# The attention steps of a two-layer hybrid block start inside its projection, with transposed probability tiles and row-group scores

## The reference

```python
h = rmsnorm(x, norm_mix[l]); proj = h @ w_in[l]                 # 15 chunks of 128 columns in the kernel
ua, cq, ckv, kr, qc, kc, vc, ud = split(proj)
ya = conformer_conv(ua, ...)     # gate, 31-tap causal depthwise conv, layernorm, silu, matmul
yb = mla(cq, ckv, kr, ...)       # 4 heads: q (96 wide) from cq, k and v from ckv, causal softmax
yc = diff_attention(qc, kc, vc, ...)  # 4 heads, each two maps of 32 columns:
#   sc = q.k * scale + bias(head, distance); a = softmax(sc); p = a[map 0] - lam * a[map 1]; p @ v; rmsnorm
yd = multiscale_pool(ud, ...)    # windows of 2, 4, 8, 16
x = x + concat(ya, yb, yc, yd) @ w_out[l]
x = x + memory_cross_attention(rmsnorm(x), mem, ...)   # k = m @ wk and v = m @ wv need mem alone
x = x + conv_glu_ffn(rmsnorm(x), ...)
```

## Time and profile before

| what | us |
|---|---|
| median of 3 runs | 1741.35 (1737.64 to 1742.45) |
| the profiled execution's own time | 1740.95 |
| its span, first to last instruction | 1739.2 |
| mean granted TensorE clock | 0.977 |
| PE busy | 1626.3 (94%) |
| DVE busy | 1104.0 (63%) |
| ACT busy | 706.7 (41%) |
| POOL busy | 235.1 (14%) |

### The profile page before, as it was taken

The page is one execution under the profiler, slowest core; times in us unless marked ns, Lnnn a source line. Parts: engine busy times, 40 slices in busy tenths (PEclk is TensorE's granted clock), DMA queues, the critical chain, the costliest instruction groups (busy, mean ns, idle before and its releaser), DMA issues. The chain is left out here.

```text
span 1739.2 us, 22473 instructions
## 1 busy us (share of the span) xinstructions
PE 1626.3 (94%) x7664; PEld 1279.8 (74%) x7664; DVE 1104.0 (63%) x1604; ACT 706.7 (41%) x1082; POOL 235.1 (14%) x212
## 2 busy tenths in 40 slices
PE   6889989889999999999998999988999999999996
PEld 3567687668767888888876768657867788888874
DVE  8967974775445764764764886485444674575575
ACT  3232345763334432432442335674243442342343
POOL 5510511112012000000020150112102000000002
PEclk9889999999999999999998999999999999999998
DMA  3143133322212233323224224241211333332323
GB/s 135 47 155 97 61 121 98 103 67 89 81 36 86 97 95 93 96 94 95 94 86 134 83 73 132 78 129 52 94 49 63 95 97 96 97 96 90 99 80 109
DMA packets 50048, 159.69 MB, mean 92 GB/s; under 512 B 6576, under 2 KB 6832, under 8 KB 49072
## 3 DMA queue, kind: packets, MB, share of 16 engines
q1 hardware_dynamic: 49968, 158.63, 29.4%
HBM read 144.97 MB, written 7.34 MB: 88 GB/s over the span
## 5 line engine op out<-in xcount | busy, mean ns | idle before, releaser
L675 ACT ACTIVATE wh<-raw 128x1024 fp32r<-128x1024 f32 x246 | 260.9, 1061 | 657.5 <-PE psum L1235 646.3
L1233 PE MATMUL psum<-a_hi,wh 128*128 128x512 f32 x1072 | 423.1, 395 | 7.8 <-DVE wl L927 7.2
L927 DVE TENSOR_TENSOR wl<-raw,wh 128x1024 fp32r<-128x1024 f32 x246 | 302.7, 1231 | 189.6 <-ACT wh L675 189.4
L1234 PE MATMUL psum<-a_lo,wh 128*128 128x512 f32 x1072 | 419.6, 391 | 0.0
L1235 PE MATMUL psum<-a_hi,wl 128*128 128x512 f32 x1072 | 419.1, 391 | 0.0
L1233 PE MATMUL psum<-b_hi,wh 128*128 128x512 f32 x608 | 239.7, 394 | 5.6 <-DVE wl L927 2.5
L1233 PEld LDWEIGHTS psum<-a_hi,wh 128*128 128x128 f32 x1072 | 202.6, 189 | 56.8 <-DVE wl L927 12.2
L1234 PE MATMUL psum<-b_lo,wh 128*128 128x512 f32 x608 | 236.7, 389 | 0.0
L1235 PE MATMUL psum<-b_hi,wl 128*128 128x512 f32 x608 | 236.7, 389 | 0.0
L1234 PEld LDWEIGHTS psum<-a_lo,wh 128*128 128x128 f32 x1072 | 202.8, 189 | 43.1 <-issue 1.4
L1235 PEld LDWEIGHTS psum<-a_hi,wl 128*128 128x128 f32 x1072 | 202.7, 189 | 42.7
(11 more groups left out here) (209 smaller groups left out, 2145.3 us busy)
## 6 DMA issues: line engine op xcount, KB each, us to landing
raw<-in_w_main SPq DMA_DIRECT2D x106, 512.0 KB, 3.5
raw<-in_w_up SPq DMA_DIRECT2D x88, 512.0 KB, 3.5
raw<-in_w_down SPq DMA_DIRECT2D x32, 512.0 KB, 3.5
bias<-bias_scratch SPq DMA_DIRECT2D x32, 256.0 KB, 2.9
terms<-qk SPq DMA_DIRECT2D x48, 128.0 KB, 2.5
raw<-in_w_last SPq DMA_DIRECT2D x16, 384.0 KB, 3.0
bias_scratch<-stage SPq DMA_DIRECT2D x64, 64.0 KB, 1.6
raw<-in_w_first SPq DMA_DIRECT2D x6, 512.0 KB, 3.6
```

The source lines that it names most:

```text
L675: act.activation(wh[:, b].rearrange("p k m -> p (k m)")[:, 0:width], raw[:, b, 0:width], ACT.Copy).then_inc(w_hi, 1)
L927: dve.tensor_tensor(wl[:, b].rearrange("p k m -> p (k m)"), raw[:, b, :], wh[:, b].rearrange("p k m -> p (k m)").bitcast(F32), ALU.subtrac ...
L1233: pe.matmul(out_ap, wh[:, b, k, :], his[:, k, :], start=(begin and i == 0), stop=False)
L1234: pe.matmul(out_ap, wh[:, b, k, :], los[:, k, :], start=False, stop=False)
```

## The change

The loop of steps becomes `STEPS` = 38 long and starts right after the small products, which now follow chunk 10. `CHUNK_AT` says which chunk closes a step: projection chunks 11 to 14 in steps 0 to 3, memory keys 15 to 22 in steps 5 to 12, memory values 23 to 30 in steps 16, 18, 20, 22, 24, 27, 30 and 33. The memory split moves into step 4. `diag` goes: POOL multiplies the whole probability tile by the inverse sum in place, and PE transposes it with the identity, three steps after the scores (`TURN_LAG`). The differential scores are two float32 matmuls of 32 rows, each map at its own row group; `terms`, the DMAs that filled it and the splits by ACT (L712) and POOL (L616) go. POOL gets the window sums after tiles 3 and 5, the differences after 4 and 6, and the `wl` of six chunks. The taps of the convolution are 20 in the projection, 8 between the query heads, 34 in steps 0 to 10. The bias tiles lie in four buffers of which two are `ssum` and `rbc`, and their loads stand between those of chunks 26 to 33.

```diff
+CHUNK_AT = {**{t: 11 + t for t in range(4)}, **{t: 10 + t for t in range(5, 13)},
+            **{t: N_WV + i for i, t in enumerate((16, 18, 20, 22, 24, 27, 30, 33))}}
+POOL_LO = {15: 25, 17: 26, 19: 27, 21: 28, 23: 29, 26: 30}
+TURN_LAG = 3
+STEPS = 38
...
-        qk, qc_at = sb("qk", [P, 8, S], F32R)
+        qk, qc_at = sb("qk", [P, 4, S], F32)
+        ptr, _ = sb("ptr", [P, 4, 4, P], F32)
+        dring, _ = sb("dring", [P, 8, S], F32, a_at + 16384)
+        bias = [bias01[:, 0, :], bias01[:, 1, :], ssum[:], rbc[:]]
...
 # POOL
+                    def lower(n):
+                        pool.wait_ge(w_hi, n + 1)
+                        pool.wait_ge(w_lo, n)
+                        pool.tensor_tensor(wl[...n % 2], raw[:, n % 2, :], wh[...n % 2], ALU.subtract).then_inc(w_lo, 1)
                     for u in range(32):
-                        if u >= 4:
-                            pool.wait_ge(t_full, u - 3)
-                        pool.wait_ge(rec_in, u + 1)
-                        pool.tensor_scalar(diag[:, u % 4, :], ident, rec[:, m:m + 1], None, ALU.mult).then_inc(diag_in, 1)
+                        if u < 16:
+                            pool.wait_ge(rec_in, u + 1)
+                            e, m = ering[:, u % RING, :], u
+                        else:
+                            pool.wait_ge(p_ready, u - 16 + 1)
+                            e, m = dring[:, 2 * u % 8, :], 2 * u - 16
+                        pool.tensor_scalar(e, e, rec[:, m:m + 1], None, ALU.mult).then_inc(scaled_in, 1)
+                        if u in (3, 5):
+                            window_sums(u // 2 - 1)
+                        if u in (4, 6):
+                            window_differences(u // 2 - 2)
+                        if u in POOL_LO:
+                            lower(POOL_LO[u])
...
 # ACT, at the end of a step
+                        n = CHUNK_AT.get(t)
+                        if n is not None:
+                            hi(n + 2)
...
 # DVE
-                    for n in range(15):
+                    for n in range(11):
...
+                        if n == 8:
+                            latents(0)
+                            latents(1)
                         if n >= 3:
-                            convolve({9: 1, 10: 1, 14: 2}.get(n, 3))
+                            convolve({8: 0, 9: 1, 10: 4}.get(n, 3))
+                    for h in range(4):
                         dve.tensor_tensor(qm(h), v_wait(f"uq{h}"), rope[:], ALU.mult).then_inc(v_dve, 1)
                         convolve(2)
...
+                        if t < 4:
+                            convolve(4)
+                        elif t > 4:
+                            convolve(3)
+                        if t == 4:
+                            for k in range(KT):
+                                dve.wait_ge(m_hi, k + 1)
+                                dve.scalar_tensor_tensor(meml[:, k, :], memf[:, k, :], ...).then_inc(m_lo, 1)
...
+                        if n is not None:
+                            if n < N_WK:
+                                scaled(n, places[n])
+                            if n + 2 not in POOL_LO.values():
+                                lo(n + 2)
...
 # PE
-                    gemms(0, 10, a_hi, a_lo, S, "in", lead=2)
+                    gemms(0, 9, a_hi, a_lo, S, "in", lead=2)
...
-                    gemms(10, 4, a_hi, a_lo, S, "in")
-                    gemm(14, 0, a_hi, a_lo, free="in")
+                    gemm(9, 1, a_hi, a_lo, free="in")
+                    gemm(10, 0, a_hi, a_lo, free="in")
...
-                            last = pe.matmul(TR[u % 2][:, P * kb:P * kb + P], e[:, P * kb:P * kb + P], diag[:, u % 4, :],
-                                             start=True, stop=True)
+                            last = pe.transpose(TR[u % 2][:, P * kb:P * kb + P], e[:, P * kb:P * kb + P], ident)
...
-                                bank_seen(k)
-                                pe.matmul(SC[k % 2], terms[h % 3][0:96, m, qb * P:qb * P + P],
-                                          terms[h % 3][0:96, 2 + m, :], start=True, stop=True).then_inc(s_full, 1)
+                            bank_seen(2 * t - 15)
+                            for m in range(2):
+                                rows = slice(64 * (h % 2) + 32 * m, 64 * (h % 2) + 32 * m + 32)
+                                pe.matmul(SC[m], qk[rows, h // 2, qb * P:qb * P + P], qk[rows, 2 + h // 2, :],
+                                          start=True, stop=True).then_inc(s_full, 1)
+                        if TURN_LAG <= t < 32 + TURN_LAG:
+                            turn(t - TURN_LAG)
...
+                        if t >= 5 and t % 2 == 1 and t <= 35:
+                            weighted_pair((t - 5) // 2)
+                        n = CHUNK_AT.get(t)
+                        if n is not None:
+                            if n < N_WK:
+                                gemm(n, n % 2, a_hi, a_lo, free="in")
+                            else:
+                                gemm(n, n % 2, memh, meml, M, ...)
                         if t == 34:
                             gemm(N_OUT, 1, b_hi, b_lo, free="act", tiles=Y_TILES[0:3], ready=y_ready, end=False)
+                        if t == 35:
+                            gemm(N_OUT, 1, b_hi, b_lo, tiles=Y_TILES[3:6], ready=y_ready, begin=False, end=False)
+                        if t == 36:
+                            gemm(N_OUT, 1, b_hi, b_lo, tiles=Y_TILES[6:7], ready=y_ready, begin=False, end=False)
+                        if t == 37:
+                            gemm(N_OUT + 1, 0, b_hi, b_lo, free="act", tiles=Y_TILES[0:7], end=False)
```

More of the change, by code:

```diff
@@ L97 @@
 V_BANK = {name: i % 2 for name, i in V_AT.items()}
-V_BANK.update({"vx1": 0, "vx2": 0, "vx3": 0, "ln_mean": 0, "mla0": 1, "ln_var": 0, "pw0": 0, "mla1": 1, "pw1": 0,
-               "diff0": 1, "sub0": 0, "diff1": 1, "sub1": 0})
+V_BANK.update({name: int(name in ("mla0", "mla1", "diff0", "diff1"))
+               for name, i in V_AT.items() if V_AT["pool0"] <= i <= V_AT["sub1"]})
 V_BEFORE = {}
@@ L705, in _ @@
                         act.activation(sqx[:, i, :], sqx[:, i, :], ACT.Sigmoid).then_inc(gate_out, 1)
-                    for n in range(3, 15):
+                    for n in range(3, 11):
                         hi(n + 2)
-                        if n >= 8 and n < 12:
-                            act.wait_ge(g_dve, n)
-                            src, dst = ((0, 2), (1, 3), (6, 4), (7, 5))[n - 8]
-                            act.activation(qk[:, dst, :], qkf[:, src, :], ACT.Copy).then_inc(qk_h, 1)
                         if n == 7:
@@ L1028, in _, with negatives @@
[L1028 to L1030 removed]
                         convolve(2)
[L1033 to L1037 removed]
+                    def negatives(m, dst, add, scale):
                         dve.wait_ge(s_full, m + 1)
[L1040 to L1043 removed]
+                        dve.tensor_tensor_reduce(dst, SC[m % 2], add, -scale, 3e38, ALU.add, ALU.min,
@@ L1294, in _ @@
                         last.then_inc(v_full, 1)
-                    for i in range(2):
-                        ps = bank(f"vc{i}")
-                        for kb in range(4):
-                            last = pe.transpose(ps[:, P * kb:P * kb + P], vct[:, i, kb * P:kb * P + P], ident)
-                        last.then_inc(v_full, 1)
-                    gemm(15, 1, memh, meml, M, "in", ready=lambda i: pe.wait_ge(m_lo, i + 1))
-                    gemm(16, 0, memh, meml, M, "in")
-                    gemms(N_WK, KT, memh, meml, M, "act", lead=2)
                     def bank_seen(m):
@@ new lines, in _ @@
+                                pe.matmul(SC[m], qk[rows, h // 2, qb * P:qb * P + P], qk[rows, 2 + h // 2, :],
+                                          start=True, stop=True).then_inc(s_full, 1)
+                        if TURN_LAG <= t < 32 + TURN_LAG:
+                            turn(t - TURN_LAG)
+                        if t == 4:
+                            pe.wait_ge(g_dve, 13)
+                            for i in range(2):
+                                ps = bank(f"vc{i}")
+                                for kb in range(4):
+                                    last = pe.transpose(ps[:, P * kb:P * kb + P], vct[:, i, kb * P:kb * P + P], ident)
+                                last.then_inc(v_full, 1)
@@ new lines, in _ @@
+                        if t in (8, 12):
+                            i = t // 4 - 2
+                            pe.wait_ge(ud_done, 2 * i + 2)
+                            product(f"pool{i}", (sw[:, SW_POOL + P * i:SW_POOL + P * i + P], ud[:, i, PPAD:]))
+                        if t == 10:
+                            pe.wait_ge(acc_done, 2)
+                            product("ln_mean", (ones, acc[:, 0, :]), (ones, acc[:, 1, :]))
+                        if t == 14:
+                            pe.wait_ge(cent_sq, 2)
+                            product("ln_var", (ones, sqx[:, 0, :]), (ones, sqx[:, 1, :]))
```

335 lines of the change are left out of this document (148 added, 187 removed).

## The result

The kernel after takes **1760.81 us** (median of 4 runs, 1756.38 to 1762.12), the kernel before 1739.69 (4 runs of the same session, 1737.64 to 1742.45): a ratio of 1.0116, interval 1.0091 to 1.014. It is slower by 1.2%, where I had forecast 1719 and a range up to 1754.

What follows compares the result with a forecast made beforehand. PE was taken to bound the stretch's first half, the chain over DVE its second. Terms summed to 199.4 us a layer against 211.3 and 209.9, together 22.4 less than 1740.95, so 1719 as the median; range 1684 to 1754.

Steps and rivals of the forecast that it cites:

- (a): From the end of chunk 8 to the first scores: 33 us, small products lasting 19 instead of 17.
- (b): Steps 0 to 3: 26 us, each 0.9 + 5.44 plus one turn, DVE's 5.9 just under PE's 6.35.
- (c): Steps 4 and 5 to the end of chunk 15: 11.4 us, of which PE works 7.8, behind DVE's memory split.
- (d): Steps 6 to 12: 45 us, PE's 37.7 plus some 7 us of waiting for POOL's tile 7.
- (e): Steps 13 to 15, which hold no chunk: 3 us each, 9 us.
- (f): Steps 16 to 33: 73.5 us, ten steps without a chunk at 2.8, eight with one at 4.6, plus smaller terms.
- (g): Steps 34 and 35: a turn, a pair and six tiles of chunk 31; less those tiles, 1.5 us.
- rival of serial row groups: The two 32-row scores run one after the other, 2.0 instead of 1.1: 29 us together, 1748, slower; chance 0.15.
- allowance: In steps 16 to 33: table changes on ACT and four reciprocals of 0.94 on DVE, together 5 us.
- The last chain: At the kernel's last pair: norm and a reciprocal of 3.35, said to have about the cover it had.
- The clock: Rival: in the short steps PE is granted 1.2 instead of 2.4 GHz, 26 us together, 1745; chance 0.03.
- The turn: In the steps: four transposes at 0.44 us replace a turn by `diag` at 0.90, 32 turns per layer.

Runs made afterwards that it cites:

- the run with the five moves: Kernel after with vc copies before memh's, Silu in step 20, chunk 30 in step 32, window work and ln_mean later, four taps behind query heads: 1715.6 us, ratio 0.9854.

## Why the prediction was wrong

Step by step in the first layer, forecast and measured:

| term | stretch | forecast | measured |
|---|---|---|---|
| (a) | to the first scores | 33 | 35.6 |
| (b) | steps 0 to 3 | 26 | 25.8 |
| (c) | steps 4, 5 | 11.4 | 15.5 |
| (d) | steps 6 to 12 | 45 | 45.7 |
| (e) | steps 13 to 15 | 9 | 9.6 |
| (f) | steps 16 to 33 | 73.5 | 81.8 |
| (g) | the last pair | 1.5 | 1.6 |
| | sum | 199.4 | 215.6 |

(81.8 us run to the end of chunk 30 at 375.0; (g) is 3.6 less the 2.0 of moved tiles.) The miss is 16.2 us, and another 5 behind the last pair. The second layer misses by 19 in all, the rest of the kernel by 1.6: together 42.

**What was right.** The price of each new instruction. Four transposes 0.44; the two row-group scores 1.05 to 1.06 against 1.1, at once. The forecast's rival of serial row groups is out, and the run with row groups alone shows no cost. On the change of tiling mode the Trainium skill (TensorEngine Tiling (Array Packing), Key Properties) says that it drains the engine; whatever that costs is inside the 1.06. POOL's scaling, which I bounded by 2.1 and 1.1, is this (shortest, median, longest in ns), the kernel after:
```profile
L673 POOL TENSOR_SCALAR ering<-ering,rec x32: 1562/1880/2063, 206.4 to 1118.5; 128x512 f32<-128x512 f32 x32
L673 POOL TENSOR_SCALAR dring<-dring,rec x32: 1562/1563/1567, 302.3 to 1190.4; 128x512 f32<-128x512 f32 x32
```
Beside the taps 2.1 held as the upper end; alone it takes 1.56, not 1.1. The steps' periods held too: one without a chunk 300.36 - 297.69 = 2.67 (I had 2.8), the next with a chunk 304.88 - 300.36 = 4.5 (4.6). Two of my sums were off by little: the terms of (f) add to 73, not 73.5, and the chances to 0.73, 0.08 and 0.19, not 0.74, 0.08 and 0.18.

**What failed is the single waits, and what I made of the clock behind them.**

(c), 4.1 us: I had the memory split limited by DVE, and did not ask what is queued behind `memh`'s copies on ACT. It is the copies of `vc`, and the first pair waits for them 5.2 us.

(f), 8.3 us: "table changes on ACT and four reciprocals of 0.94 on DVE together 5, an allowance; steps 32 and 33 have no scores, -3". The allowance was not placed anywhere. The waits are 2.21 at the pair of step 19 (ACT's Silu and its table loads stand ahead of `mla1`'s eviction), 3.50 in step 33, and four smaller of 0.4 to 1.3; 9.5 us in all against the 2 of my net. Step 33 is the plain error: with neither scores nor a chunk ahead of the turn, the chain over POOL is bare, and I booked it as a gain. Moving one chunk by one step brought 12 us.

(a), 2.6 us: the query head waits 1.79 for DVE, behind the four taps. I did count that; what I didn't count is that 10.2 us behind it run at 0.50.

The last chain, 5 us: "has about the cover it had". It waits 1.8 and 1.6 for DVE where the kernel before waits 0.9, and its stage is at 0.92.

(d) came out right for half a reason: I had 7 us of waiting for POOL; it is 2.96 for POOL and 2.98 for `acc` behind it, with 6.8 us of half clock on top.

**The clock.** I gave it 0.03, as something that many short steps might do. The short steps did not: from 330.9 to 361.5 us, with steps down to 2.67 us, the clock is 1.00. It falls at the long single waits, and can then cost more than the wait: 1.8 us of waiting in (a) cost 5.3. It falls towards their end or shortly behind it. Here PE has not yet started again (the waits for `vc` and for `dring`):
```profile
230.40:231.20 0.80, 0.00 (x1) 0.03 (x1) 0.80 (x3) 0.65 (x2) 0.00 (x0) 0.50 0.00 0
366.90:367.70 0.80, 0.00 (x0) 0.00 (x0) 0.73 (x4) 0.00 (x0) 0.80 (x1) 0.50 0.00 0
```
That is how the removal of 10.5 us of idle per layer could bring 22 per layer, and work in the gaps 20 us. The windows bound it for the first layer: 29 us more at half clock than before, so at most 14.5 us. The page of the Trainium skill that I cited (TensorE: Matmul & The Clock Gate, Part 4: PE-mode transpose) would blame the transposes. The trace disagrees in two ways: 279.7 to 311.8 us of the run with the five moves, full of transposed turns, are granted 1.00, and filling the waits of the kernel after with matmuls restores the clock while every transpose stays.

**The turn.** The term was 32 x 0.46 per layer, the main gain of the forecast. As a price on PE it is right, and it never reached the end: beside the stalls the transposed turn does not gain and costs up to 10 us (7 by the ratios, and part of it clock that the exchange does not touch), without them it gains and costs nothing, and alone, in the old order with two steps of distance, it costs 32. I had assumed that PE bounds the first half and the chain the second. With the scaling of 1.56 to 2.06 us in it instead of 0.60, the chain grows by 1.0 to 1.5 us per tile, and what PE saves comes back as waits and lower clock on the same schedule. What was not tried is the transposed turn with its scaling somewhere else than on POOL.

So of the change's three parts the row groups are neutral, the turns cost up to 10 us as placed, and the longer pipeline (the run with diagonal turns is the change without them) costs 11 against the kernel before. Five small moves against the stalls bring 35 us with diagonal turns and 45 with transposed ones. With these the kernel is some 24 us faster than before; that this is near my 1719 is luck, since the turns, the main term of that sum, bring nothing in it. The prices were right and a list of waits was missing.

## What to carry to other kernels

When work is moved to fill one engine, list per engine the order of what it has to issue around every seam (the first use of a bank, the last step without cover, a block on ACT or POOL ahead of a short copy that PE needs), and give each wait a place; an allowance without a place is a wait not found. Here two single waits of PE cost two to three times their length (1.8 us cost 5.3 in the stage up to the first scores; 2.6 us less of waiting in the last steps brought 6 a layer), so look at the granted clock of the stage before reading its busy time. Remove such waits together: taken one at a time they partly hide each other. And a cheaper instruction on the busy engine that makes the chain to it longer gains nothing until a run has shown that the chain has room.

## What the runs showed of the hardware

- With its waits filled PE is granted 0.99 in the first layer's 239 us, where the same program with seven waits of 1.8 to 5.2 us has 0.91; added matmuls on constants made the kernel 20 us faster.
- The lower clock lasts on when PE works again, and the loss can exceed the wait: 10.2 us at 0.50 behind a wait of 1.79, 6.8 behind one of 2.21. It does not follow every such wait: behind the 1.79 in the second layer of the run with diagonal turns the clock stays at 1.00, and the stage takes 32.2 us instead of 35.6.
- POOL's in-place scaling of 128x512 float32 takes 1.56 us in the second half of the steps and up to 2.06 in the first, beside DVE's taps, which read two tiles from SBUF. The Trainium skill (SBUF — State Buffer, Who interferes with whom) says that such DVE instructions contend with POOL's reads; the trace agrees, with these two numbers.
- Two float32 matmuls of 32 rows and 512 columns in different row groups run at once: 1.06 us for both, where one of 128 rows takes 0.905.
